# Two chained blocks in one kernel: where the later modulation groups of the first block stand

## The reference

```python
mod_x = silu(c) @ w_ada[l] + b_ada[l]          # 1024 -> 6144, likewise mod_c from c_ctx
sh1, sc1, g1, sh2, sc2, g2 = split(mod_x, 6)
h = layer_norm(x) * (1 + sc1) + sh1
p = h @ w_in[l]                                 # keys, queries, fourier input, three gates
mix = (g_f * y_f + g_m * y_m + g_g * y_g) @ w_o # y_m, y_g: two attentions of 8 heads
x = layer_norm(alpha * x + g1 * mix, ln1_g, ln1_b)
m = layer_norm(x) * (1 + sc2) + sh2
x = layer_norm(alpha * x + g2 * (relu(m @ w1) ** 2 @ w2), ln2_g, ln2_b)
```

## Time and profile before

| what | value |
|---|---|
| median of 3 runs | 3157.55 us (3156.21 to 3159.61) |
| the profiled execution | 3166.1 us, span 3164.3 us |
| granted TensorE clock, mean | 0.956 |
| TensorE / POOL / ScalarE / VectorE busy | 93% / 57% / 40% / 31% |
| moved by DMA | 422.57 MB, mean 134 GB/s |

### The profile page before, as it was taken

One profiled execution on the slowest core, in us unless ns is written; L12 is line 12 of the kernel. 1 busy time (PEld: TensorE's weight loads), 2 busy tenths in 40 slices (PEclk: granted clock), 3 DMA queues, 4 the chain that ended last, 5 costly groups with the idle time before them and its releaser, 6 DMA issues.

```text
span 3164.3 us, 48951 instructions
## 1 busy us (share of the span) xinstructions
PE 2929.7 (93%) x20289; PEld 2597.7 (82%) x20289; DVE 982.4 (31%) x1694; ACT 1270.2 (40%) x1683; POOL 1805.0 (57%) x1380
## 2 busy tenths in 40 slices
PE   6889888998999989999898999899999999899999
PEld 4676667766878748679898999898999998889999
DVE  1223232233112252342325323134331224144331
ACT  0523533214222143453443444455444434454443
POOL 1310214414454223258587797865998897865896
PEclk8989988998999988999999999999999999999999
DMA  7314222342322253345354556533555556533553
GB/s 228 79 44 145 67 92 69 93 131 83 105 82 95 91 133 93 121 125 168 107 174 159 167 179 169 168 120 112 175 180 180 169 184 173 162 120 117 173 180 129
DMA packets 397397, 422.57 MB, mean 134 GB/s; under 512 B 74566, under 2 KB 367422, under 8 KB 396935
## 3 DMA queue, kind: packets, MB, share of 16 engines
q1 hardware_dynamic: 397224, 420.06, 42.8%
HBM read 418.96 MB, written 3.16 MB: 133 GB/s over the span
## 4 chain that ended last, share of the span: by engine, by line
PE 81%; DVE 6%; POOL 6%; ACT 3%; DMA 2%; issue 2%; SPq 0%; DVEq 0%; POOLq 0%; ACTq 0%
PE ps L786 62%; PE ps L770 16%; POOL ring_r L1458 6%; PE ps L813 2%; ACT ring_hi L1491 1%; DVE arena L2233 1%; DMA ring<-in_w_ada 1%; DVE stat L2219 1%; DVE arena L2111 0%; ACT arena L1532 0%; DMA arena<-in_bucket_of_block 0%; PE ps L827 0%; DVE arena L2116 0%; DMA ring<-in_w_branch_gla 0%; DMA ring<-in_w_in 0%
## 5 line engine op out<-in xcount | busy, mean ns | idle before, releaser
L1458 POOL TENSOR_TENSOR ring_r<-ring,ring_hi 128x512 fp32r<-128x512 f32 x1376 | 1804.8, 1351 | 1336.0 <-ACT ring_hi L1491 1335.7
L786 PE MATMUL ps<-hT_r,ring_hi 128*128 128x256 f32 (+1 forms) x6176 | 1149.7, 309 | 73.1 <-DVE hT_r L2119 31.2
L786 PEld LDWEIGHTS ps<-hT_r,ring_hi 128*128 128x128 f32 x6176 | 930.9, 195 | 138.9 <-issue 51.0
L1491 ACT ACTIVATE ring_hi<-ring 128x2048 fp32r<-128x2048 f32 x344 | 654.9, 1910 | 367.4 <-DMA ring<-in_w 114.7
L786 PE MATMUL ps<-hT_r,ring_r 128*128 128x256 f32 (+1 forms) x3088 | 696.8, 307 | 0.0
L786 PE MATMUL ps<-arena_r,ring_hi 128*128 128x256 f32 (+1 forms) x3728 | 636.6, 312 | 21.3 <-DVE arena_r L2307 9.7
L786 PEld LDWEIGHTS ps<-arena_r,ring_hi 128*128 128x128 f32 x3728 | 536.0, 191 | 71.0 <-issue 26.1
L786 PEld LDWEIGHTS ps<-hT_r,ring_r 128*128 128x128 f32 x3088 | 510.7, 195 | 24.2
L786 PE MATMUL ps<-arena_r,ring_r 128*128 128x256 f32 (+1 forms) x1864 | 355.7, 310 | 0.0
L786 PEld LDWEIGHTS ps<-arena_r,ring_r 128*128 128x128 f32 x1864 | 280.4, 190 | 20.6
L770 PE MATMUL ps<-arena 128*64 128x128 f32 (+9 forms) x1616 | 203.7, 372 | 21.0 <-DVE arena L2196 11.9
(11 more groups left out here) (226 smaller groups left out, 2267.2 us busy)
## 6 DMA issues: line engine op xcount, KB each, us to landing
ring<-in_w_in SPq DMA_DIRECT2D x82, 1024.0 KB
ring<-in_w SPq DMA_DIRECT2D x64, 1024.0 KB
ring<-in_w_ada SPq DMA_DIRECT2D x48, 1024.0 KB
ring<-in_ffn_w_up SPq DMA_DIRECT2D x44, 1024.0 KB
ring<-in_ffn_w_gate SPq DMA_DIRECT2D x44, 1024.0 KB
ring<-in_ffn_w_down SPq DMA_DIRECT2D x44, 1024.0 KB
ring<-in_w_in SPq DMA_DIRECT2D x48, 256.0 KB
ring<-in_w_o SPq DMA_DIRECT2D x8, 1024.0 KB
```

The source lines that it names most:

```text
L786: last[t] = pe.matmul(o, lhsT, rhs, start=start and j == 0, stop=stop and j == n - 1, skip_group_check=True)
L1458: ins = pool.tensor_tensor(k.ring_lo[s][:, part], k.ring[s][:, part], k.ring_hi[s][:, part], ALU.subtract)
L1491: act.activation(k.ring_hi[s][:, :], k.ring[s][:, :], ACT.Copy).then_inc(k.hi_ready[s], 1)
```

## The change

The eight groups that stood in the norms are moved into the attentions: layer 0's m gets steps 13 and 15 beside the six it had, its g has six groups (1, 3, 5, 8, 13, 15) instead of two, and layer 1's two attentions have four and two instead of three and one. The last turns move to g16 and g6. All fillers of the norms are gone. `RING` and SP's order follow. The splits ahead of their use (`AHEAD_M`, `AHEAD_G`, and those at the gate steps of layer 0 and the fourier steps of layer 1) get new places: the four gate panels of layer 0 are split in m16, g1, g3 and g5, the next two in g7 and g9, as before, and the two for the branches in g16 and g17 instead of g14 and g15. In layer 1, the splits stand in m8, m9, g0, g1, g5, g6, g7 and g8, instead of m6, m7, g0, g1, g4, g5, g6 and g8. The number of instructions of each kind and of bytes stays as it was, but for the order of small scales in VectorE.

```diff
-RING = "a" * ADA_FIRST + "d" * 10 + "a" * 12 + "dddd" + "aa" + "dd" + "aa" + "d" * 16 + "a" * 8 + "d" * 32 + "a" * 8 \
-    + "d" * 10 + "a" * 6 + "dddd" + "aa" + "d" * 18 + "d" * 32
+RING = "a" * ADA_FIRST + "d" * 10 + "a" * 16 + "daa" * 4 + "dd" + "a" * 4 + "d" * 48 \
+    + "d" * 10 + "a" * 8 + "dddd" + "a" * 4 + "d" * 50
...
-MODS_M, MODS_G, MODS_LAST = ((4, 6, 8, 10, 12, 14), (2, 4, 6)), ((8, 13), (4,)), (14, 5)
-AHEAD_M, AHEAD_G = ((13, 15), (6, 7)), ((7, 9, 14, 15), (4, 5))
+MODS_M, MODS_G, MODS_LAST = ((4, 6, 8, 10, 12, 13, 14, 15), (2, 4, 6, 7)), ((1, 3, 5, 8, 13, 15), (4, 5)), (16, 6)
+AHEAD_M, AHEAD_G = ((16,), (8, 9)), ((1, 3, 5, 7, 9, 16, 17), (5, 6, 7, 8))
...
@@ SyncE: order of the panels
-                def gates(g, n):
+                def gates(g, n, fill=None):
                     for j in range(2):
                         s = slot()
                         c0 = GATE0 + g * D + n + j * 256
                         load(s, [(at(s, 0, KD, 256), w_in[:, :, c0:c0 + 256])])
+                        if fill is not None:
+                            modulations(fill + 2 * j, 2)
...
-                if l == 0:
-                    modulations(24, 8)
...
-            modulations(32, 8)
...
@@ TensorE: the norms (ScalarE and VectorE likewise)
-                norm(slice(0, TOK), x_moved if l == 0 else None, (l, 0))
-                if l == 1:
-                    modulated_last()
+                norm(slice(0, TOK), x_moved if l == 0 else None)
...
-                norm(cols, last_results(), (1, 2) if fill else (0, 0))
-                norm(cols, None, (fill, 0))
-                if fill:
-                    modulated_last()
+                norm(cols, last_results())
+                norm(cols, None)
                 mlp(l, cols)
-                norm(cols, last_results(), (1, 2) if fill else (0, 0))
+                norm(cols, last_results())
...
@@ ScalarE, attention
                     if kind == "g" and u in gate_steps(l):
-                        if u in gate_steps(l)[:2]:
+                        if l > 0 and u in gate_steps(l)[:2]:
                             split()
...
                     if kind == "g" and u in fourier_steps(l):
-                        if l > 0:
-                            split()
                         skip(4)
```

More of the change, by code:

```diff
@@ L618, in out_of @@
                          if name == "w_go" else [(v, rows(W[name][lay])[:, :, n:n + 512])])
[L620 to L623, removed]
+                modulations(*((8, 16) if l == 0 else (36, 8)))
+                for n in (0, 1):
+                    gates(0, 512 * n, 24 + 4 * n if l == 0 else None)
+                if l == 1:
+                    modulations(44, 4)
                 for n in (0, 512):
@@ L626, in mix_and_mlp @@
                 if l == 0:
-                    modulations(22, 2)
+                    modulations(32, 4)
                 for n in (0, 512):
@@ L1150, in _ @@
                 mix_out(cols)
-                fill = l == 0
-                norm(cols, last_results(), (1, 2) if fill else (0, 0))
-                norm(cols, None, (fill, 0))
-                if fill:
-                    modulated_last()
+                norm(cols, last_results())
+                norm(cols, None)
                 mlp(l, cols)
-                norm(cols, last_results(), (1, 2) if fill else (0, 0))
+                norm(cols, last_results())
             h2 = k.h2
@@ L1507, in modulation, with norm @@
                 act.activation(k.mod_rows[group % 2], ps[:, b, :], ACT.Copy).then_inc(k.bank_read[b], 1)
-            def norm(centred, cols, affine=None, fill=(0, 0), last=False):
+            def norm(centred, cols, affine=None, fill=(0, 0), ahead=False):
                 n = cols.stop - cols.start
@@ L1523, in norm @@
                     modulate()
-                if last:
-                    modulated_last()
+                if ahead:
                     split()
@@ L1772, in _ @@
                 fill = l == 0
-                norm(plain, slice(0, TOK), modulated(mod + SC1, mod + SH1, (0, 1)), (l, 0), not fill)
+                norm(plain, slice(0, TOK), modulated(mod + SC1, mod + SH1, (0, 1)), ahead=not fill)
                 if l == 1:
@@ L1781, in _ @@
                 mix_out(l, cols)
-                norm(k.xT, cols, None, (1, 2) if fill else (0, 0))
-                norm(plain, cols, modulated(mod + SC2, mod + SH2, halves), (fill, 0), fill)
+                norm(k.xT, cols, None)
+                norm(plain, cols, modulated(mod + SC2, mod + SH2, halves), ahead=fill)
                 if fill:
@@ L2247, in attention @@
                         modulations()
-                        scales((l * MODS + SC2,))
+                        scales((l * MODS + SC2,) + ((MODS + SC1,) if l == 0 else ()))
                     modulations()
@@ L2331, in _ @@
                 fill = l == 0
-                norm(plain, slice(0, TOK), None, "h_ready", (l, 0), not fill)
+                norm(plain, slice(0, TOK), None, "h_ready")
                 project(l, cols)
@@ L2344, in _ @@
                 dve.wait_ge(*k.moved(T.last()))
[L2345 to L2348, removed]
+                norm(k.xT, cols, gained("ln1", l), "x_ready")
+                norm(plain, cols, None, "h_ready")
                 x = k.xT[:, :, cols]
@@ L2373, in _ @@
                 dve.wait_ge(*k.moved(T.last()))
-                norm(k.xT, cols, gained("ln2", l), "x_ready" if l == 0 else "y_ready", (1, 2) if fill else (0, 0))
+                norm(k.xT, cols, gained("ln2", l), "x_ready" if l == 0 else "y_ready")
             dve.memset(chain, 1.0)
```

## The result

The changed kernel takes 3170.10 us (median of 6 runs, 3165.98 to 3174.19), the kernel before 3158.34 us (6 runs, 3152.76 to 3160.58). The ratio is 1.0040, 95% interval 1.0027 to 1.0053: slower by 11.8 us. The forecast was 3169.2 us, slower by 11.7.

The account below looks back on a forecast made before the run. TensorE, 81% of the chain that ended last, was taken as the bound. Terms -3.2 +21.8 -3.0 -3.6 -0.3 gave +11.7 us on the median 3157.55: 3169.2 us, range 3153 to 3181, the forecast's own 3163 to 3180.

Parts of the forecast that it names:

- the large term: Layer 0's second attention: late gate panel splits make TensorE wait, +21.8 us.
- gates, first projection's start to fourth's end: Layer 0's second attention: three waits for late panels +17.8 us, half clock in the projections +4.0, together +21.8.
- norms behind mixer and MLP: Layer 0's norms without groups: x sums start sooner, -7.2 us, slower squares sums +4.0, together -3.2.
- end of the first attention: Layer 0, m13 to m16: scaling free of POOL, first gate panel ready sooner, -3.0 us.
- end of the second attention: Layer 0, g15 to g17: group fills a wait, scaling free of POOL, branches sooner, -3.6 us.
- layer 1: First attention's end -3.0 us, fourier panel split in g5 waits and meets half clock +2.7, together -0.3.
- DMA: Panel transfers in the attentions: no byte added, tightest panels hidden by 2 us; otherwise 0 to 5 us lost.
- Rival three: Three gate waits under 3 us each, the idle is the gain: 3150 us and below; chance 0.14.
- The groups add nothing: Layer 0's second attention: three new groups, 3.0 us each, vanish inside the gate panel waits.
- The rival in which the clock decides: Four norm sums at half rate, three gate projections with 8 us: 3175.6 us; chance 0.1, within the slower case's 0.66.

Follow-up runs that it names:

- e0: The kernel before, unchanged, profiled a second time: 3158.06 us, span 3156.3 us.
- e1: The changed kernel with layer 0's second to fourth gate panels split one step earlier (g0, g2, g4): ratio 0.9982 to the kernel before.
- e2: The kernel before, groups unmoved, with only layer 0's gate panels split late (m16, g1, g3, g5): ratio 1.0052 to the kernel before.
- e9: The changed kernel with the splits of g1, g3, g5 put ahead of that step's Exp in ScalarE's program: ratio 0.9999 to the kernel before.
- e7: The changed kernel, late gate splits kept, three groups of g1, g3, g5 put back in layer 0's mixer norm: ratio 1.0038 to the kernel before.
- e4: The changed kernel with gate splits in g0, g2, g4 and three groups put back in layer 0's mixer norm: ratio 0.9969 to the kernel before.
- e3: The changed kernel, late gate splits kept, with the first branch panel split in g14, not g16: ratio 1.0021 to the kernel before.
- e5: The changed kernel with gate splits in g0, g2, g4 and branch panels split in g14 and g16: ratio 0.9945 to the kernel before.
- e8: The kernel before, groups unmoved, with layer 0's gate panels split in m16, g0, g2, g4: ratio 0.998 to the kernel before.

## Why the prediction was right

The mechanism and the large term were right. That the total, +11.7 against a measured +11.8, agrees to 0.1 us is luck: the terms miss by more than that in both directions, and the profiles have differences that no step priced. By the prediction's own steps, the profile after against each of the two profiles of before:

| step | predicted, us | against before, us | against e0, us |
|---|---|---|---|
| gates, first projection's start to fourth's end | +21.8 (18 to 26) | +20.9 | +25.3 |
| norms behind mixer and MLP | -3.2 (-9 to +3) | -3.8 and -3.1 | -3.8 and -3.3 |
| end of the first attention | -3.0 | -3.7 | -6.0 |
| end of the second attention | -3.6 | +0.2 | +1.3 |
| layer 1 | -0.3 | -5.4 | -3.5 |
| DMA | 0 (to 5) | no wait of TensorE for it in either attention | |
| branches and output of the mixer | no term | +0.9 | +0.9 |
| MLP of layer 0 | no term | -3.6 | -3.6 |
| all else | no term | +2.0 | +5.0 |
| whole profile | +11.7 | +4.3 | +12.3 |

The lines are rounded, and the layer 1 line runs from the second sum of squares behind the MLP to the sum of x behind layer 1's mixer. The steps that the prediction priced come to +5.1 us against the one profile and +10.0 against the other. Of "all else" 1.5 and 4.5 us lie ahead of the first attention's fourth step, where nothing was changed: in the twelve profiles that step's transposes start anywhere between 242.5 and 248.2 us.

**The gates: right, by its mechanism.** From one projection's end to the next one's start it is 11.4, 12.5 and 12.1 us for 11.2, 12.3 and 12.3. That is 18.6 us more than in the profile before, for 17.8 predicted. The three projections took 12.66, 13.55 and 12.86 us by the chain, not 13.6 each: +2.4 over the earlier trace rows instead of +4.0 (13.6 less the lengths in the earlier trace rows would be 4.1). Against e0, whose projections ran almost at full clock, the same three are 5.7 us longer. So the size of this term hangs on the profile that it is measured from, and +4.0 lies between the two. e1 and e2 show that these late splits are the whole of the slowdown and more, and e9 shows that it is the place behind Exp and copy in ScalarE's program that makes 2.5 to 3.1 us of each. Rival three needed waits under 3 us each; they were 6.8, 5.6 in two pieces and 5.1.

**"The groups add nothing": right here, wrong as a rule.** They add 1.4 us beside the late splits, 6.9 beside early ones (e7, e4).

**The norms: the starts right, the squares a matter of the execution.** The sums of x start 2.7 and 3.6 us sooner after their squares (2.8 and 3.8 predicted), run 0.7 and 0.8 us shorter, and 0.4 us is gained behind each. Against it the prediction set 1.0 for each of four sums of squares. In the profile after one of four ran slow, +1.7 in all; that is 2.3 of the 3.7 us by which the norms gave more, the shorter sums of x are the rest. But the profiles of e1, e3, e5 and e9 have the same norms, and there three, three, two and one of the four ran slow, 5.0, 5.1, 3.4 and 1.7 us. The mean of the five is 3.4, near the 4.0 of the prediction. From its first sum to the MLP, the norm behind the mixer is 50.4 and 50.5 us long in two of the five (after, e9), 53.5 in e5, 55.0 in e1 and 55.1 in e3, against 54.3 in all four profiles with the groups in it (before, e0, e2, e8); the one behind the MLP, to layer 1's first matmuls, is 52.2 in all five, against 52.8 to 55.5. By the means that is -1.4 and -2.4, -3.8 for -3.2 predicted; the -6.9 of the profile after owes 3.1 us to its execution. The rival in which the clock decides wanted four slow sums, and none of the five profiles has more than three. The Trainium skill, "TensorE: Matmul & The Clock Gate", section "What's actually happening", has the halved clock as the default that activity lifts; for an equal gap of 2.33 us the runs show both outcomes (7.11 and 8.80), so the direction stands. A price by that sentence alone, four slow sums of 1.6 us, would by estimate be 6.4 us, more than any of the five profiles shows.

**The end of the first attention: right.** From the transposes of the fourth step to the first projection it is 95.6 us for 99.3 before (101.6 in e0); the first projection waits 1.57 us for the panel split in m16, as the step said it would wait. That the splits make the gain, and not the groups, is shown by e2 and e8.

**The end of the second attention: this step failed.** It forecast the branches 3.6 us sooner. Two of its links held. The group fitted into the 3.46 us wait of the earlier trace rows: the two transposes are 8.53 us apart, 8.17 before, so it cost 0.4 us where the step had counted on a gain of 0.6. And the next transposes came 3.45 us sooner (3.68 behind the former ones, 7.13 before), about half of it by VectorE's scaling, which took 0.88 us without POOL for 2.61 beside it, and half by the full clock of the matmuls between (1.07 and 1.09 us for 1.97 and 1.98). The third was wrong, the readiness of the panel. ScalarE's split began at 506.83 and POOL's subtractions at 508.84, and they took 7.06 us and not 5.03. Three of the four took 1.27 to 1.31 us each; the fourth began beside VectorE's first long instruction and took 3.32. In the timeline of POOL (five instructions of a window, then the fourth alone) and of VectorE:

```profile
508.84 10.34 POOL L1453 TENSOR_TENSOR ring_r<-ring,ring_hi 128x512 fp32r<-128x512 f32 x5 [54.14 <-ACT ring_hi L1486]
...
512.58 3.32 POOL L1453 TENSOR_TENSOR ring_r<-ring,ring_hi 128x512 fp32r<-128x512 f32 x1
```

```profile
511.82 0.42 DVE L2202 COPY arena<-ps 128x256 f32<-128x256 f32 x1 [2.80 <-PE ps L770]
512.16 2.61 DVE L2276 TENSOR_SCALAR xT<-xT 128x4096 f32<-128x4096 f32 x1
514.69 6.64 DVE L2279 TENSOR_TENSOR arena_r<-arena,arena_r 128x2048 fp32r<-128x2048 f32 x2
```

VectorE's long instructions of the branches, which had stood behind POOL's panel before, now stand beside it. The prediction counted what POOL takes from VectorE and forgot what VectorE takes from POOL. TensorE began the branches after 4.24 us of waiting, at 515.95:

```profile
515.95 1.65 PE L786 MATMUL ps<-hT_r,ring_hi 128*128 128x512 f32 x3 [4.24 <-POOL ring_r L1453]
```

The tail itself gained 1.2 us and 1.4 were lost ahead of it, beside the fourier projections. Of the 3.8 us between forecast and profile, 1.4 are this loss, 0.9 the later transposes and 1.5 the panel: 2.0 by POOL, less 0.5 because the split came sooner than counted. e3 takes the wait away, and its branches begin 3.4 us sooner behind the fourth projection than in the profile before, which is what the step had promised.

**Layer 1: undersized.** From the second sum of squares behind the MLP to the sum of x in layer 1's norm behind its mixer, four profiles with the old places of this layer (before, e0, e2, e8) have 357.6 to 360.2 us, mean 358.7, and eight with the new ones 354.8 to 357.6, mean 355.9: 2.8 us. The same twelve profiles show the two terms apart. From the squares of the layer's first norm to the first gate projection, the end of its first attention, it is 85.8 to 86.6 us with the old places and 81.6 in all eight with the new: -4.5, where -3.0 was forecast. From there to the branches it is 72.3 to 72.7 us and 74.5: +1.9, where +2.7 was forecast. The loss is at the fourier projection, which takes 8.28 us for 5.95 behind a wait of 3.11 us:

```profile
1384.38 1.23 PE L786 MATMUL ps<-arena_r,ring_hi 128*128 128x256 f32 x4 [3.11 <-POOL ring_r L1453]
```

It does not start later behind the gate projections than before (20.2 us for 20.3 to 20.8), so the wait itself adds nothing and the half clock is the whole loss. Why the end of the first attention gave 1.5 us more than forecast was not tried.

**Not settled:** how much of e5's gain in the branches is the edit's and how much is where the half clock fell, and whether moving the groups of the norms behind the MLP is worth anything by itself: that norm is 52.2 us in every profile without them and 52.8 to 55.5 with them, but the totals don't resolve it. That would need timing finer than the 0.15% of these intervals.

## What to carry to other kernels

When work is moved between stages, count the things that are moved along with it: here eight groups of filler changed hands for little, and three weight preparations that lost the cover of the projection before them made the whole difference. For each preparation, add up what stands in front of it in its engine's own program from the moment its input is free, and compare that with the cover of the step before; a preparation one use ahead was enough (e8), one without that cover cost a wait each time, and its place within the step decided 2.5 to 3.1 us of each (e9). A filler is free only where the wait exists: once the preparation was early, the same groups cost the stretch 6.9 us. And before a small term is called hit or missed by one profile, look for the same stretch in other profiles of the same program: here a norm varied by 4.7 us between them.

## What the runs showed of the hardware

- Four subtractions of 512 columns on POOL took 4.95 to 5.43 us for the gate panels. For the first branch panel they took 7.06 us, all of the difference in the one that began beside VectorE's instruction over 4096 columns (3.32 us for 1.27), and 9.12 us for the second, beside VectorE's instructions over 2048 columns. The slowing goes both ways: VectorE's scaling took 0.88 us alone and 2.61 to 2.75 beside POOL.
- The half clock behind a short gap is not decided by the gap. Behind 2.33 us without a matmul, and a sum of x at full rate ahead of it, the 16 matmuls of the squares took 7.11 us in one norm of the changed kernel and 8.80 in another. Behind 6.04 us the 16 matmuls took 8.68 and 8.70 in it, and 9.87 in e1. It is not only chance either: in the eight profiles without groups in the norm behind the MLP, the first squares there took 8.8 us each time and the second 7.1, while the two behind the mixer changed from profile to profile.
- Two profiles of the same kernel, 3156.3 and 3164.3 us long, differ by 4.4 us in one stretch of 60 us, 3.5 of it by projections that ran partly at half clock in one and hardly in the other. A difference of a few microseconds between two single profiles needs the waits beside it before it can be read as an effect.
